# All modulation blocks of a two-layer mixed-attention network on VectorE, in a one-core Trainium2 kernel

## The reference, cut to what matters

```python
c_act = silu(c)
for l in range(2):
    mod = c_act @ ada_w[l] + ada_b[l]              # ada_w[l]: 1024 x 6144
    sh_m, sc_m, g_m, sh_f, sc_f, g_f = split(mod, 6)
    h = rmsnorm(x, norm_mix[l]) * (1 + sc_m) + sh_m
    proj = h @ w_in[l]
    # q, k, v -> differential attention; ml -> latent attention; z, xbc, dt -> state space branch; gates
    x = x + g_m * (merged_branches @ w_out[l])
    h = rmsnorm(x, norm_ffn[l]) * (1 + sc_f) + sh_f
    x = x + g_f * (gated_convolved_ffn(h))
```

## Time and profile before

| | |
|---|---|
| median of 3 runs | 2156.21 us (2152.43 to 2161.04) |
| profiled execution | 2151.73 us, span 2149.9 us |
| TensorE busy | 1951.4 us, 91% |
| VectorE busy | 674.3 us, 31% |
| ScalarE busy | 414.7 us, 19% |
| GpSimd busy | 186.6 us, 9% |
| DMA | 456.96 MB, mean 213 GB/s |
| granted TensorE clock, mean | 0.952 |

### The profile page before, as it was taken

One profiled execution on the slowest core, in us unless ns is written; L12 is line 12 of the kernel. 1 busy time (PEld: TensorE's weight loads), 2 busy tenths in 40 slices (PEclk: granted clock), 3 DMA queues, 4 the chain that ended last, 5 costly groups with the idle time before them and its releaser, 6 DMA issues.

```text
span 2149.9 us, 22335 instructions
## 1 busy us (share of the span) xinstructions
PE 1951.4 (91%) x9032; PEld 1396.4 (65%) x9032; DVE 674.3 (31%) x1092; ACT 414.7 (19%) x874; POOL 186.6 (9%) x159
## 2 busy tenths in 40 slices
PE   4879999889999798999989999997879999999976
PEld 1458688778888447778777888855754444444443
DVE  3355226442232426225542223332141111111111
ACT  2143311202110124312202110014210111011101
POOL 0384000000000357100000000000000000000000
PEclk9889999999999899999999999997879999999988
DMA  9455333283446465434344444742339999999950
GB/s 350 143 196 196 118 118 118 79 273 118 157 157 229 143 214 178 142 132 137 118 157 157 157 157 177 279 175 78 118 133 420 416 416 422 416 414 412 423 242 20
DMA packets 151830, 456.96 MB, mean 213 GB/s; under 512 B 8880, under 2 KB 58288, under 8 KB 137648
## 3 DMA queue, kind: packets, MB, share of 16 engines
q1 hardware_dynamic: 149024, 450.37, 55.9%
q10 hardware_dynamic: 2704, 5.16, 0.8%
HBM read 453.68 MB, written 1.84 MB: 212 GB/s over the span
## 4 chain that ended last, share of the span: by engine, by line
PE 85%; DVE 6%; ACT 5%; issue 2%; DVEq 1%; DMA 1%; ACTq 0%
PE acc L715 33%; PE acc L1133 11%; PE acc L725 9%; PE aux L1149 6%; PE acc L989 4%; PE aux L989 4%; PE acc L1121 3%; PE acc L1012 3%; PE aux L638 3%; PE acc L1157 2%; PE aux L1157 1%; PE acc L1090 1%; PE aux L654 1%; ACT area L1228 1%; ACT yT L1228 1%
## 5 line engine op out<-in xcount | busy, mean ns | idle before, releaser
L715 PE MATMUL acc<-hT,ring 128*128 128x256 f32 x2688 | 594.9, 383 | 6.9 <-ACT hT L1302 6.9
L715 PEld LDWEIGHTS acc<-hT,ring 128*128 128x128 f32 x2688 | 515.4, 192 | 82.6 <-ACT hT L1302 7.7
L725 PE MATMUL acc<-ring,hT 128*128 128x512 f32 (+1 forms) x384 | 167.1, 595 | 18.3 <-ACT hT L1302 18.3
L1133 PE MATMUL acc<-ring,yT 128*64 128x512 f32 x528 | 176.3, 594 | 2.1 <-ACT yT L1228 2.1
L1604 POOL TENSOR_TENSOR zb<-ring,cact 128x512 f32<-128x512 f32 x80 | 89.6, 1125 | 671.1 <-DMA ring<-in_ada_w 603.8
L725 PEld LDWEIGHTS acc<-ring,hT 128*128 128x128 f32 x384 | 73.9, 194 | 105.1 <-issue 81.1
L2028 DVE SCALAR_TENSOR_TENSOR area<-acc,cc,area 128x255 f32<-128x255 f32 (+1 forms) x176 | 72.7, 475 | 214.1 <-ACT area L1470 212.5
L2257 DVE TENSOR_TENSOR xT<-xT,acc 128x1024 f32<-128x1024 f32 x17 | 20.8, 1221 | 339.5 <-PE aux L1157 339.5
L1133 PE MATMUL acc<-area,yT 128*64 128x512 f32 x432 | 126.7, 593 | 0.0
L638 PE MATMUL aux<-kc,area 128*128 128x128 f32 (+1 forms) x412 | 66.0, 310 | 65.7 <-DMA area<-in_x 15.9
L638 PEld LDWEIGHTS aux<-kc,area 128*128 128x128 f32 (+1 forms) x412 | 54.5, 158 | 78.1 <-DMA area<-in_x 15.9
(11 more groups left out here) (359 smaller groups left out, 2195.5 us busy)
## 6 DMA issues: line engine op xcount, KB each, us to landing
ring<-in_w_in SPq DMA_DIRECT2D x34, 2048.0 KB, 9.2
ring<-in_ada_w SPq DMA_DIRECT2D x28, 2048.0 KB, 9.4
ring<-in_ffn_w_up SPq DMA_DIRECT2D x44, 1024.0 KB, 7.6
ring<-in_w_down SPq DMA_DIRECT2D x18, 2048.0 KB, 13.1
ring<-in_w_gate SPq DMA_DIRECT2D x17, 2048.0 KB, 9.2
ring<-in_w_up SPq DMA_DIRECT2D x16, 2048.0 KB, 12.9
area<-in_w_up SPq DMA_DIRECT2D x14, 2048.0 KB, 15.5
area<-in_w_gate SPq DMA_DIRECT2D x13, 2048.0 KB, 12.3
```

The lines of the kernel that those rows point to most:

```text
L715: mm = pe.matmul(acc[LU.buf[use]][:, SEQ * j:SEQ * j + SEQ], w[:, k, c0:c0 + P], x[:, k, :], start=(k == 0), stop=(k == n - 1))
L725: mm = pe.matmul(acc[LU.buf[use]][:, at:at + width], x[:, k, P * t:P * t + P], w[:, k, :], start=(k == 0), stop=(k == n - 1))
L1133: mm = pe.matmul(dst[CAP * e:CAP * e + CAP, :], xg[:, b, k, CAP * e:CAP * e + CAP], w[:, k, :], start=(k == 0), stop=(k == KT - 1))
```

## The change

GpSimd computes no modulation block any more; its loop is gone, with the semaphore `part_pool`. VectorE calls `ada` for all twelve: 4 and 5 right behind `scale_x`, ahead of the norm of q and k; 6 behind that norm; 7, 8 and 9 behind L1924 of the first three convolution chunks; 10 and 11 where they were. The partial sums of blocks 7, 8 and 9 lie in `ysT`, since `zb` holds z by then. TensorE's column sums move accordingly: 4 behind `k`, 5 behind `v`, 6 behind `ml`, 7 behind `xbc2`, 8 behind `xbc3`, 9 behind `bb0`. The additions of `ada_b` (L1878, `gmh`) move behind the state space branch. `LAYER_CHUNKS` puts the modulation chunks at the places where VectorE comes to need them; `ml` and `uqkv` are each asked for one chunk later than before, and `ada7`, `ada8`, `ada9` stand between the `xbc` chunks.

```diff
@@ LAYER_CHUNKS @@
-LAYER_CHUNKS = (["q", "k", "ada4", "v", "ml", "ada5", "uqkv", "ada6", "ga0", "ada7", "ga1", "gb0", "ada8", "gb1",
-                 "z0", "z1", "ba"] + [f"xbc{i}" for i in range(4)] + ["bb", "gc0", "gc1", "bc0", "ada9", "bc1", "ada10",
+LAYER_CHUNKS = (["q", "k", "ada4", "v", "ada5", "ml", "ada6", "uqkv", "ga0", "ga1", "gb0", "gb1", "z0", "z1", "ba",
+                 "xbc0", "ada7", "xbc1", "ada8", "xbc2", "ada9", "xbc3", "bb", "gc0", "gc1", "bc0", "bc1", "ada10",
                  "wo0", "ada11", "wo1"] + [f"up{i}" for i in range(11)]
...
-ADA_POOL = 5
@@ buffers @@
-        *partial, product = [zb[:, i // 2, 512 * (i % 2):512 * (i % 2) + 512] for i in range(4)]
+        partial = [zb[:, i // 2, 512 * (i % 2):512 * (i % 2) + 512] for i in range(3)]
+        partial_ssm = [shaped(ysT.rearrange("p h n -> p (h n)"), 4, 512)[:, i, :] for i in range(3)]
...
+            return partial_ssm[n] if i in (7, 8, 9) else partial[n]
@@ TensorE @@
                 token_chunk("k")
+                ada(4)
                 token_chunk("v")
+                ada(5)
                 token_chunk("ml", ML_W + SM_H)
-                ada(4)
+                ada(6)
...
-                ada(5)
...
-                    if n < 2:
-                        ada((6, 7)[n])
                 gate_pieces("gb1", 0, 4)
-                ada(8)
...
                 gate_pieces("xbc2", 0, 4)
+                ada(7)
...
                 gate_pieces("xbc3", 0, 4)
+                ada(8)
...
                     feature_piece("bb0", j, w, P * j, yT[:, 4:8, :])
+                ada(9)
...
-                ada(9)
                 ada(10)
@@ GpSimd @@
-            pool.wait_ge(c_ready, 1)
-            with pool.Fori(0, DEPTH) as l:
-                for n, i in enumerate(ADA_ORDER[:ADA_POOL]):
...
-                    times(part, 0)
-                    for k in range(1, KT):
-                        times(product, k)
-                        pool.drain()
-                        last = pool.tensor_tensor(part, part, product, ALU.add)
...
-                    last.then_inc(part_pool, 1)
-                    pool.drain()
@@ VectorE @@
                 scale_x(amix)
+                ada(4)
+                ada(5)
 
                 freed("q")
                 freed("k")
...
                     D_()
+                ada(6)
 
                 dve.wait_ge(ml_rt, l + 1)
...
-                dve.wait_ge(ada_done, 12 * l + ADA_AHEAD + ADA_POOL)
-                tt(mod[:, 16:36], pmod[:, 16:36], cc[:, V_ADA + 16:V_ADA + 36], ALU.add)
...
                     stt(part, th, 1.0, part, ALU.add, ALU.mult).then_inc(xb_ready, 1)
+                    if c < 3:
+                        ada(7 + c)
...
-                ada(9)
+                dve.wait_ge(ada_done, 12 * l + ADA_AHEAD + 6)
+                tt(mod[:, 16:40], pmod[:, 16:40], cc[:, V_ADA + 16:V_ADA + 40], ALU.add)
+                D_()
+                ts(gmh, mod[:, 16:24], 0.5, None, ALU.mult)
                 freed("gc0")
```

More of the change, by code:

```diff
@@ L327, in program, with partial_of @@
         sqx = view(8704, KT, SEQ)
-        *partial, product = [zb[:, i // 2, 512 * (i % 2):512 * (i % 2) + 512] for i in range(4)]
+        partial = [zb[:, i // 2, 512 * (i % 2):512 * (i % 2) + 512] for i in range(3)]
+        partial_ssm = [shaped(ysT.rearrange("p h n -> p (h n)"), 4, 512)[:, i, :] for i in range(3)]
+        def partial_of(i):
+            n = ADA_ORDER.index(i) % 3
+            return partial_ssm[n] if i in (7, 8, 9) else partial[n]
         xin = view(0, T, D)
@@ L428, in program @@
         dn_done = sem("dn_done")
-        part_ready, part_pool = sem("part_ready"), sem("part_pool")
+        part_ready = sem("part_ready")
         ada_done = sem("ada_done")
@@ L477, in part_of @@
         def part_of(i):
-            n = ADA_ORDER.index(i)
-            return (part_pool, n + 1, ADA_POOL) if n < ADA_POOL else (part_ready, ADA_AHEAD + n + 1 - ADA_POOL, 12 - ADA_POOL)
+            return part_ready, ADA_AHEAD + ADA_ORDER.index(i) + 1, 12
         def release_of(name):
@@ L659, in ada_sum @@
                 pe.wait_ge(signal, value)
-                part = partial[ADA_ORDER.index(i) % 3]
+                part = partial_of(i)
                 for j in range(4):
@@ L1593, in _ @@
             pool.memset(epsc[:, 1:2], 1.0).then_inc(fill, 1)
-            pool.wait_ge(c_ready, 1)
-            with pool.Fori(0, DEPTH) as l:
-                for n, i in enumerate(ADA_ORDER[:ADA_POOL]):
-                    slot, value = LAYER_RING[f"ada{i}"]
-                    pool.wait_ge(landed[slot], l * LAYER_LANDED[slot] + value)
-                    pool.wait_ge(ada_done, l * 12 + ADA_AHEAD + n - 2)
-                    w, part = shaped(ring[:, slot, :], KT, 512), partial[n % 3]
-                    times = lambda dst, k: pool.tensor_tensor(dst, w[:, k, :], cact[:, k:k + 1].to_broadcast([P, 512]), ALU.mult)
-                    times(part, 0)
-                    for k in range(1, KT):
-                        times(product, k)
-                        pool.drain()
-                        last = pool.tensor_tensor(part, part, product, ALU.add)
-                        if k < KT - 1:
-                            pool.drain()
-                    last.then_inc(part_pool, 1)
-                    pool.drain()
         @block.vector
@@ L1674, in ada_partial @@
                     dve.wait_ge(ada_done, before - 2)
-                w, part = shaped(ring[:, slot, :], KT, 512), partial[ADA_ORDER.index(i) % 3]
+                w, part = shaped(ring[:, slot, :], KT, 512), partial_of(i)
                 ts(part, w[:, 0, :], cact[:, 0:1], None, ALU.mult)
@@ L1876, in _ @@
                 tt(heads, heads, bc(sso.rearrange("p t h -> p (t h)"), 2, 2 * DA_D), ALU.mult).then_inc(oa_n, 1)
-                dve.wait_ge(ada_done, 12 * l + ADA_AHEAD + ADA_POOL)
-                tt(mod[:, 16:36], pmod[:, 16:36], cc[:, V_ADA + 16:V_ADA + 36], ALU.add)
-                D_()
-                ts(gmh, mod[:, 16:24], 0.5, None, ALU.mult)
                 for n in range(3):
@@ L2014, in _ @@
                         dve.wait_ge(ada_done, 12 * l + 12)
-                        tt(mod[:, 36:48], pmod[:, 36:48], cc[:, V_ADA + 36:V_ADA + 48], ALU.add)
+                        tt(mod[:, 40:48], pmod[:, 40:48], cc[:, V_ADA + 40:V_ADA + 48], ALU.add)
                         D_()
```

## The result

The changed kernel takes **2139.58 us** (median of 4 runs, 2136.65 to 2142.55), the kernel before beside it 2157.14 (2152.43 to 2161.04): ratio 0.992 [0.9894, 0.9945], 17.6 us less. The profiled executions differ by 15.1 us: 2136.65 with a span of 2134.8, against 2151.73 and 2149.9. Forecast was 2134 in a range of 2125 to 2147.

The account below looks back on a forecast made before the run. The chain was taken as 85% TensorE, with time lost where GpSimd slows VectorE and TensorE waits. Terms 3.9 + 3.2 + 2.6 + 8.4 + 4.6 - 0.5 = 22.2 us, from the median 2156.2 to 2134; range 2125 to 2147.

Parts of the forecast that it names:

- Head of layer 1: L1744 to L1756 in layer 1: VectorE falls from 6.27 to 2.4 us without GpSimd, gaining 3.9 us; bounds 2.5 to 3.9.
- Clock: Behind the first attention unit's shortened gaps TensorE's granted clock holds, speeding gate pieces and transposes: 4.6 us, bounds 0 and 4.6.
- rival A: The clock falls all the same in the shortened gaps and 4.6 us don't come: 2138.6 us; chance 0.22.
- First attention unit: TensorE's idle time for VectorE's slowed result shrinks to about 3 us: 4.7 and 3.7, 8.4 us in both layers.
- Latent vectors and dt: ScalarE's idle time for L1800, ahead of copies `uqkv` waits for, shrinks: 1.5 and 1.1, 2.6 us in both layers.
- Column sums: TensorE's moved sums cost the same eight narrow matmuls at every place, or stand where it waits anyway: 0.
- First tile: From L1771 to ScalarE's first shift, small VectorE instructions and the first scaled tile come faster: 3.2 us for both layers.
- Blocks 4 to 6 and SyncE's queue: These blocks fit VectorE's waits and later-requested chunks land in time: 0 each; bounds for the queue 0 and -3 us.
- rival C: Slower: VectorE and ring close a loop in the convolution, each waiting for the other: 2169 us; chance 0.04.
- Blocks 7 to 9: Between convolution chunks VectorE's 6.28 us blocks just fit its 6.37 us rests: -0.5 us for both layers, bounds 0 and -3.
- Rival D: VectorE's slow stretches come from something else (DMA writes into SBUF), so neither relief nor loss: 2156 us; chance 0.05.
- B: Half the relief is taken by what is late next, and the convolution's blocks cost some: 2146 us; chance 0.12.

Follow-up runs that it names:

- e1: Changed kernel with GpSimd given back five blocks per layer of products and additions that nobody reads: 2154.3 us, ratio to the kernel before 1.0003.
- e2: Kernel before, order and ring untouched, with GpSimd computing one product per block (seven of eight row tiles left out): 2133.83 us, ratio 0.9905.
- e7: Changed kernel with the first attention unit's fourth gate piece run ahead of TensorE's wait for VectorE's result: 2129.15 us, ratio to before 0.991.
- e11: Changed kernel with VectorE's and ScalarE's layer loops written out, the fourth gate piece ahead of its wait, sums 4 and 5 behind `ml`: 2111.61 us, ratio 0.9816.
- e10: Changed kernel with the column sums of blocks 4 and 5 moved from behind `k` and `v` to behind `ml`: 2136.14 us, ratio to before 0.9925.
- e3: Changed kernel with only the first product of blocks 4 to 8 left on VectorE: 2138.83 us in a single run.
- e9: Changed kernel with 2.4 us of useless VectorE additions ahead of block 8, between convolution chunks: 2139.33 us in a single run.
- e12: The changed kernel itself, unaltered, timed on another chip: 2139.25 us, ratio to the kernel before 0.9949.
- e4: Changed kernel with three extra VectorE additions of 128x1024 between L1737 and L1739 at the head of each layer: 2144.14 us in a single run.
- e6: Changed kernel with VectorE's and ScalarE's loops over the layers written out: 2126.15 us, ratio to the kernel before 0.9899.
- e13: Kernel before with one product per GpSimd block, again, on the same chip as e12: 2135.99 us, ratio 0.9923.

## Why the prediction was right, and where its terms failed

The direction, the mechanism and the range were right: GpSimd's work beside VectorE was paid on the path (`e1`). Of the sum of 22.2 us, two terms worth 8.5 did not come.

- **Head of layer 1, forecast 3.9: 0.** From the last addition to x to L1756, now L1739, it was 13.66 us (715.68 to 729.34) and is 13.61. The instructions did become shorter, by just what was forecast. The step that failed is "ScalarE's exponential, its square root and `invert_root` stand behind it, so the difference comes out whole": I asked for what is late next on ScalarE only, with table loads as the lower bound of 2.5, and took VectorE itself for ready. It wasn't: the stream of instructions is next, and the slow instructions had run inside its wait. From L1727 to the end of L1739 it is 5.70 us, where the sign of being right was 2.4. The row was there to see: 6.02 us of "issue" ahead of L1744 in the earlier trace rows, absent in layer 0, which I compared with layer 1 as if only GpSimd told them apart.
- **Clock, forecast 4.6: about 0.** The gate piece takes 5.59 and 5.14 for 4.70 and 5.42, the transposes 1.12 and 0.66 for 1.12 twice. That is rival A. "The remaining gaps are of that length" failed first: they are 3.83, not 3.05. Half a microsecond less would hardly have saved it (slow behind seven of eight gaps of 3.46 to 3.48), and `e2` shows that it would not have held for certain at 2.6 either. The term was also a little large for its own words: half of 1.12 is 0.56 and not 0.7, which makes 4.3. In the changed kernel a stretch of 3 us elsewhere, nearly without matmuls, kept the full clock, as in the earlier trace rows; its window (columns: us, PE, PEld, DVE, ACT, POOL busy, PEclk, DMA share, GB/s), beside those of the gap:

```profile
153.00:157.00 4.00, 0.18 (x1) 0.18 (x2) 2.67 (x11) 1.22 (x6) 0.00 (x0) 0.79 0.00 2
155.00:160.00 5.00, 3.18 (x10) 2.73 (x11) 4.85 (x12) 0.60 (x1) 0.00 (x0) 0.53 0.00 2
...
1376.00:1379.00 3.00, 0.04 (x1) 0.07 (x1) 2.42 (x3) 0.46 (x1) 0.00 (x0) 1.00 1.06 389
```

  One idle stretch that kept the clock was no ground for 2 of 2 others. The Trainium skill's warning against gaps of more than about 3 us ("TensorE: Matmul & The Clock Gate", the table of why it matters) deserved more than 0.22. The sure cure was a filled gap (full speed in all four layers of `e7` and `e11`), where a gap shortened to 2.6 kept the clock in three of four.
- **First attention unit, forecast 8.4: 7.1.** 4.01 and 3.05. The 3.9 of delay forecast for layer 0 was 3.3 (6.35 to 3.06); the 0.8 beyond it came nearly whole.
- **Latent vectors and dt, forecast 2.6: right at its place, lost behind it.** ScalarE's table load of L1350 now waits for nothing in either layer, and its copies L1353 follow. TensorE's two waits there, 1.48 and 2.15 us in layer 0 and 1.85 and 1.67 in layer 1, are 0.69 and 1.37, and 0.89 and 1.37: 2.8 less. But the stage as a whole grew by 1.0: two column sums more stand in it, of 0.8 us each and in both layers.
- **Column sums, forecast 0.** Over the layer this is not refuted: three sums of 0.95 us have left attention, where the stage up to `z` gained 6.2 us although the clock term failed (six sums are some 5.2 of it; in layer 0 another 1.5 are 32 transposes, 3.91 us where it was 5.38); two entered ahead of the end of `ml` and two behind `z`. But "a sum is the same eight narrow matmuls at every place: 0" hid that the place decides: behind `ml` they are nearly free, and `e10`'s stage gained 3.5 us in two layers with them.
- **First tile, forecast 3.2: right.** From `amix` (L1754) to the first matmul of `q` 1.37 less in layer 0 (2.71 to 1.34), 1.96 in layer 1 (3.29 to 1.33). In layer 0 a later start of the head (L1727 at 50.27, L1744 before at 48.81), which is scatter, ate it.
- **Blocks 4 to 6 and SyncE's queue, forecast 0: right.** No wait for a DMA is among those of TensorE or of its loads, but for `x` at the start of the program; rival C did not begin.
- **Blocks 7 to 9, forecast -0.5 for both layers: -1.0, and not by VectorE.** `z` to `bc` is 0.47 and 0.49 us longer, and neither less nor more VectorE work there changes it (`e3`, `e9`). What is left is the three column sums that stand there now; no run tested them alone.
- **Not seen**: TensorE's waits, merged in one view, between 55 and 1385 us (total, times, longest):

```profile
PE aux L641 <- DVE area L1855: 7.7, 2, 3.8
...
PE acc L718 <- DVE gates L1993: 4.0, 2, 2.0
```

  The second was 2.2 us before: 0.9 us more in each layer. One sum stands ahead of it (0.95 us) where two stood (1.84 together), so TensorE comes earlier to a result of VectorE and waits for it; a sum taken from in front of a wait is no gain. And what stands behind this wait, the matmuls of `wo0`, ran at one of two speeds. TensorE's timelines of layer 1, of the changed kernel and of `e12`, which is the same kernel:

```profile
1101.61 14.08 PE L718 MATMUL acc<-gates,ring 128*128 128x256 f32 x64 [2.02 <-DVE gates L1993]
...
1098.68 17.08 PE L718 MATMUL acc<-gates,ring 128*128 128x256 f32 x64 [2.02 <-DVE gates L1993]
```

  The granted clock of the first 5.4 us is 1.00 in the one and 0.50 in the other, 3 us more. It was slow in 11 of the 22 layers traced with the changed order, and in 1 of 6 with the order of before, too few to say that the longer wait does it. In the two traces compared in the table it is fast everywhere, so their difference lacks this cost, which the medians have in part.

Rival D falls by `e1`, C by the waits. A came true for the clock and B in one term, the head, where what was late next took all of the relief. The median came out at A's 2138.6 nearly, but not by A's sum: 3.9 us in the table are from stages that the change doesn't touch. Without them the spans would differ by 11.2 us, between the gains of the two chips, 17.6 and 9.7 in the medians. So the size was luckier than its terms. Why the kernel before was 7 to 8 us faster on two other chips (2149.17 and 2148.93) than on the first, and the changed one, timed on one of them, not, stays open.

## What to carry to other kernels

Work on GpSimd is not free because nobody waits for it: compare the same lines of VectorE with GpSimd silent and busy before calling GpSimd a spare engine, and where VectorE has quiet stretches put the work there. When a slow stretch on the path is to go, ask of its own engine too what is late next: "issue" behind a loop's jump is such a floor, and writing the loop out removed it here. And fill a gap of TensorE rather than shorten it, and put small matmuls where TensorE waits anyway.

## What the runs showed of the hardware

- Behind the jump back of a layer loop VectorE stood for 6.54 us, and again for 3.80 us nine instructions on, ScalarE for 5.20, with no result to wait for; the instruction queue q14 had two packets in each of VectorE's waits. With the loops written out the waits were gone and the way from the last addition to x to `q` in layer 1 was 10.05 us shorter. In `e4` the second wait shrank from 3.80 to 2.29 us when 1.2 us of work stood ahead of it.
- Beside a working GpSimd, instructions of VectorE at 128 columns took 0.54 to 0.64 us (`e1`) instead of 0.22 to 0.29, and a tile of 256 columns 0.81 instead of 0.41. Five such blocks per layer took 14.7 us in the medians (2154.3 against 2139.58; ratio to the kernel before 1.0003 against 0.992), 0.7 to 0.8% of this kernel.
- TensorE's granted clock fell to the lower of its levels behind 3.83 us without matmuls, in both layers (0.53 in the mean from 155 to 160 us in layer 0, 0.65 from 820 to 823 in layer 1), behind seven of eight gaps of 3.46 to 3.48 us (`e3` to `e6`) and behind one of four gaps of 2.6 us (`e2`, `e13`). Behind 2.0 to 2.2 us without matmuls, ahead of `wo0`, it was at its lower level in 11 of 22 layers.
